# Norm rows read in the PSUM banks, and two more slots in the ring of expert rows, in a two-layer diffusion backbone

## Reference, cut to what matters

```
mod = silu(cond) @ w_mod + b_mod                  # 6 rows of 1024: sh1, sc1, g1, sh2, sc2, g2, one set for P, one for S
h   = layer_norm(x) * (1 + sc1) + sh1
mix = attention of three kinds (h @ w_in) @ w_out
x   = layer_norm(alpha * x + g1 * mix, ln1_g, ln1_b)
h   = layer_norm(x) * (1 + sc2) + sh2
ff  = peer_ffn(h)                                 # per token: 8 heads x top 16 = 128 experts of 16384
x   = layer_norm(alpha * x + g2 * ff, ln2_g, ln2_b)

def peer_ffn(h):                                  # u_tab, v_tab: 16384 x 1024
    q = h @ wq; s = q . keys; experts, gates = product-key top 16 of each head
    act = gelu(h . u_tab[experts])                # 128 dot products for each token
    return sum_k (gates * act)[k] * v_tab[experts[k]]
```

## Time and profile before

| | |
|---|---|
| median of 3 runs | 2485.88 us (2480.08 to 2488.46) |
| span of the profiled execution | 2660.3 us (its time beside the span is not shown) |
| TensorE, VectorE, GpSimd, ScalarE busy | 1716.3, 1616.4, 1491.3, 337.3 us |
| bytes moved | 980.68 MB, 369 GB/s over the span |
| of these, gathers and w_mod (queue 0) | 847.35 MB, 82.1% of 16 DMA engines' time |
| mean granted TensorE clock | 0.790 |

### The profile page before, as it was taken

One profiled execution on the slowest core, in us unless ns is written; L12 is line 12 of the kernel. 1 busy time (PEld: TensorE's weight loads), 2 busy tenths in 40 slices (PEclk: granted clock), 3 DMA queues, 4 the chain that ended last, 5 costly groups with the idle time before them and its releaser, 6 DMA issues.

```text
span 2660.3 us, 24559 instructions
## 1 busy us (share of the span) xinstructions
PE 1716.3 (65%) x8433; PEld 893.7 (34%) x8433; DVE 1616.4 (61%) x3949; ACT 337.3 (13%) x998; POOL 1491.3 (56%) x1583
## 2 busy tenths in 40 slices
PE   6886759676376666366577585867638667435556
PEld 4564514342143422222344342435214342000101
DVE  3266775676865673954467964547866566854441
ACT  1320013101120100002110101311112010000000
POOL 1105466655656465566455664555665666766664
PEclk8987877888578778687688797788757878777779
DMA  8969899999999999999899999889999999999997
GB/s 315 422 252 364 314 389 367 390 370 394 368 328 401 358 411 413 404 411 410 314 366 387 369 411 355 317 336 354 410 380 328 395 379 411 389 357 377 364 367 296
DMA packets 248333, 980.68 MB, mean 369 GB/s; under 512 B 28001, under 2 KB 29681, under 8 KB 232849
## 3 DMA queue, kind: packets, MB, share of 16 engines
q0 software_dynamic: 226944, 847.35, 82.1%
q1 hardware_dynamic: 19536, 130.80, 12.3%
q10 hardware_dynamic: 1728, 0.95, 0.1%
HBM read 976.47 MB, written 2.52 MB: 368 GB/s over the span
## 4 chain that ended last, share of the span: by engine, by line
PE 17%; issue 12%; POOL 9%; DMA 8%; another core or an unknown queue 8%; DVE 7%; ACT 1%; SPq 0%; DVEq 0%; ACTq 0%; POOLq 0%
POOL expert L660 9%; PE acc L968 6%; DMA expert<-in_experts,eidx_t 4%; DVE expert L1529 3%; PE mmb L911 2%; DMA expert<-in_experts,eidx 2%; PE mmb L779 2%; PE mmb L860 1%; PE ob L887 1%; DMA wt<-in_w_wq 1%; PE trb L867 1%; PE mmb L743 1%; ACT hT L1048 1%; DVE small L1216 0%
## 5 line engine op out<-in xcount | busy, mean ns | idle before, releaser
L660 POOL DMA_INDIRECT expert<-in_experts,eidx x768 | 736.1, 958 | 648.0 <-PE acc L968 261.2
L1529 DVE CUSTOM_DVE_ANT_0 expert<-expert,hb 128x1024 f32<-128x1024 f32 x768 | 904.3, 1218 | 268.1 <-DMA expert<-in_experts,eidx 211.2
L660 POOL DMA_INDIRECT expert<-in_experts,eidx_t x768 | 730.5, 951 | 329.7 <-issue 212.5
L968 PE MATMUL acc<-expert,strip 128*32 128x512 f32 x3072 | 710.8, 725 | 262.2 <-DMA expert<-in_experts,eidx_t 190.5
L968 PEld LDWEIGHTS acc<-expert,strip 128*32 128x32 f32 x3072 | 135.0, 123 | 737.5 <-DMA expert<-in_experts,eidx_t 399.5
L911 PE MATMUL mmb<-hT,wt 128*128 128x128 f32 x1472 | 211.8, 307 | 58.2 <-issue 31.4
L911 PEld LDWEIGHTS mmb<-hT,wt 128*128 128x128 f32 x1472 | 200.3, 220 | 86.7 <-issue 68.9
L769 PE MATMUL mmb<-wt,hT 128*128 128x244 f32 x736 | 178.6, 404 | 33.4 <-issue 12.9
L769 PEld LDWEIGHTS mmb<-wt,hT 128*128 128x128 f32 x736 | 152.8, 211 | 64.6 <-issue 35.3
L1399 DVE TENSOR_REDUCE neg_max<-mmb 128x1 f32<-128x384 f32 (+1 forms) x120 | 55.1, 466 | 165.1 <-PE mmb L860 83.5
L942 PE MATMUL trb<-ident,acts 128*128 128x128 f32 x24 | 9.6, 398 | 171.0 <-DVE acts L1549 100.9
(11 more groups left out here) (192 smaller groups left out, 1629.8 us busy)
## 6 DMA issues: line engine op xcount, KB each, us to landing
wt<-in_w_wq SPq DMA_DIRECT2D x46, 1152.0 KB
expert<-in_w_mod POOLq DMA_DIRECT2D x39, 1024.0 KB, 13.8
wt<-in_w_win SPq DMA_DIRECT2D x30, 976.0 KB
wt<-in_w_wout SPq DMA_DIRECT2D x24, 1024.0 KB
expert<-in_experts,eidx POOLq DMA_INDIRECT x768
expert<-in_experts,eidx_t POOLq DMA_INDIRECT x768
wt<-in_w_mod SPq DMA_DIRECT2D x8, 1024.0 KB
wt<-in_w_uq SPq DMA_DIRECT2D x6, 384.0 KB
```

Of the source, the lines that this page charges most:

```text
L660: pool.indirect_dma_start(expert[:, g % RING, :], None, table, bass.IndirectOffsetOnAxis(at, 0)).then_inc(landed[g % RING], 16)
L968: m = pe.matmul(acc[32 * i:32 * i + 32, cs], strip[:, q % 2, i, at:at + 32], expert[:, (g + i) % RING, cs], start=k < 4, stop=False, skip_ ...
L1529: v.tensor_tensor_reduce(expert[:, r, :], expert[:, r, :], hb[:], 1.0, 0.0, ALU.mult, ALU.add, dots[:, k:k + 1]).then_inc(dot_ready, 1)
```

## The change

Three things change together.

1. `rows` and `rows_used` are gone. A `row` step of a gain, a bias or the gate g1 leaves the row in the two `mmb` banks, which are now one tensor `mm2` of 1024 columns. VectorE waits for the matmuls (`mm_full`), reads `mm2` and then frees both banks (`row_used`). So each such row stands right ahead of its reader in the list, and gain and bias are read in two steps (`ln_x` 2 and 3, `fin` 2 and 3) with a row step in front of each.
2. The gate g2 of `fin` is still copied by ScalarE, now into `tmp`, in a `row` step at the end of the weave of its own block (`gate_row`).
3. The 8 KB a partition that `rows` took go to the ring: `RING` is 17. The ring of modulation weights keeps its 7 places.

The costs that space the gathers have the split steps and 0.5 for each row.

```diff
-RING = 15
+RING = 17
-RROWS = 2
...
 def weave(l, b, side, beside=()):
+    side = with_rows(side) + [("row", l, "", b, gate_row(l, b))]
...
+def gate_row(l, b):
+    return 16 * l + 10 + int(b > 0)
 def rows_wanted(x):
-                 {("ln_x", 0): (2,), ("ln_x", 2): (6, 7), ("fin", 0): (5,), ("fin", 2): (8, 9)}.get((kind, e), ()))
+                 {("ln_x", 0): (2,), ("ln_x", 2): (6,), ("ln_x", 3): (7,), ("fin", 2): (8,), ("fin", 3): (9,)}.get((kind, e), ()))
 def with_rows(steps):
-    (places each row as early as its bank, its buffer and its modulation allow)
+    return [y for x in steps for y in [("row", x[1], "", 0, j) for j in rows_wanted(x)] + [x]]
...
-        rows = sb("rows", [P, RROWS, D])
+        mm2 = ps("mmb", [P, D])
+        mmb = [mm2[:, 512 * i:512 * (i + 1)] for i in range(2)]
...
@@ ScalarE @@
-                if kind == "row":
-                    k = n("rows") - 1
-                    if k >= RROWS:
-                        act.wait_ge(rows_used, k - RROWS + 1)
-                    for half in range(2):
-                        mm_copy(rows[:, k % RROWS, half * 512:half * 512 + 512], lambda bk: bk[:], mm + half)
+                if kind == "row" and e != gate_row(l, b):
+                    n("mm_full", 2)
+                if kind == "row" and e == gate_row(l, b):
+                    act.wait_ge(idx_ready, n("gate", 0))
+                    if l == L - 1 and b > 0:
+                        act.wait_ge(y_ready, b)
+                    for u in (mm, mm + 1):
+                        half = u % 2
+                        mm_copy(tmp[:, half * 512:half * 512 + 512], lambda bk: bk[:], u)
@@ VectorE @@
+            def affine_gain(z):
+                link(v.scalar_tensor_tensor(out=z, in0=z, scalar=small[:, 28:29], in1=row(), op0=ALU.subtract, op1=ALU.mult))
+                row_used()
+            def affine_bias(dst, z):
+                link(v.scalar_tensor_tensor(out=dst, in0=z, scalar=small[:, 30:31], in1=row(), op0=ALU.mult, op1=ALU.add))
+                row_used()
             def row():
-                k = n("row") - 1
-                v.wait_ge(mm_free, at_row[k] + 2)
-                return rows[:, k % RROWS, :]
+                v.wait_ge(mm_full, at_row[n("row") - 1])
+                return mm2[:]
+            def row_used():
+                v.sem_inc(mm_free, 2)
...
-                        r = row()
+                        v.wait_ge(mm_free, at_gate + 2)
                         v.wait_ge(slot_done, SLOTS * (3 * l + b + 1))
-                        v.tensor_tensor(z, acc[:], r, ALU.mult).then_inc(acc_read, 1)
+                        v.tensor_tensor(z, acc[:], z, ALU.mult).then_inc(acc_read, 1)
```

More of the change, by code:

```diff
@@ L76 @@
 COST = {"mod": 2.8, "madd": 1.3, "cols": 1.5, "ln1": 5.5, "h_t": 2.5, "win": 6.8, "prep": (1.2, 7, 2.6, 3), "k_t": 2, "q_t": 4, "q_rope": 1.5,
-        "qm_t": 1, "cache_t": 2, "kv_mla": 5, "heads": 2, "mix": 1, "wout": 3.6, "ln_x": (2.5, 5.2, 2.5),
-        "ln_h": 5.2, "route": 1.5, "topk": 4.7, "pick": (4.4, 6.5, 4.4, 6.5), "fin": (1.3, 6.5, 2.5), "idx_t": 1}
+        "qm_t": 1, "cache_t": 2, "kv_mla": 5, "heads": 2, "mix": 1, "wout": 3.6, "ln_x": (2.5, 5.2, 1.3, 1.3), "row": 0.5,
+        "ln_h": 5.2, "route": 1.5, "topk": 4.7, "pick": (4.4, 6.5, 4.4, 6.5), "fin": (1.3, 6.5, 1.3, 1.3), "idx_t": 1}
 def cost_of(x):
@@ L152, in block_steps @@
     out += [("wout", l, s, b, n) for n in range(OUT_T)]
-    out += [("ln_x", l, s, b, i) for i in range(3)] + [("ln_h", l, s, b, 0), ("h_t", l, s, b, 2)]
+    out += [("ln_x", l, s, b, i) for i in range(4)] + [("ln_h", l, s, b, 0), ("h_t", l, s, b, 2)]
     for n in range(WQ_T + 1):
@@ L223, in fins @@
 def fins(l, b):
-    return [("fin", l, "", b, i) for i in range(3)]
+    return [("fin", l, "", b, i) for i in range(4)]
 def early_mod(x):
@@ L243, in plan @@
                   {"k_t": 1, "kv_mla": 1, "q_t": 1, "qm_t": 2, "heads": 0.45})
-    steps += prompt[mix:project] + [("madd", 0, "", 0, 2), ("cols", 0, "", 0, 1)] + fill(prompt[project:norm], s1[1:] + s2[1:] + rest[2:4], {"ln_x": 2})
+    steps += prompt[mix:project] + [("madd", 0, "", 0, 2), ("cols", 0, "", 0, 1)]
+    steps += with_rows(fill(prompt[project:norm], s1[1:] + s2[1:] + rest[2:4], {"ln_x": 1.5}))
     steps += fill(prompt[norm:cut], rest[4:] + [("madd", 0, "", 0, 3), ("cols", 1, "", 0, 0)], {"route": 1, "topk": 0.5, "pick": 4})
@@ L279, in rows_wanted @@
     return tuple(16 * l + (2 * r + st if r < 6 else 6 + r) for r in
-                 {("ln_x", 0): (2,), ("ln_x", 2): (6, 7), ("fin", 0): (5,), ("fin", 2): (8, 9)}.get((kind, e), ()))
+                 {("ln_x", 0): (2,), ("ln_x", 2): (6,), ("ln_x", 3): (7,), ("fin", 2): (8,), ("fin", 3): (9,)}.get((kind, e), ()))
 def with_rows(steps):
[L286 to L305, removed]
+    return [y for x in steps for y in [("row", x[1], "", 0, j) for j in rows_wanted(x)] + [x]]
+STEPS = plan()
 MODS = [x for x in STEPS if x[0] == "mod"]
+for at, step in enumerate(STEPS):
+    assert step[0] != "row" or all(STEPS.index(y) < at for y in MODS if y[1] == step[4] // 16 and y[3] == step[4] % 16 // 2)
 EARLY = sum(early_mod(x) for x in MODS)
 SUMS = sum(x[0] == "madd" for x in STEPS)
-MOD_RING = RING // 2
+MOD_RING = 7
 assert all(early_mod(x) for x in MODS[:EARLY])
@@ L455, in trunk_program @@
         acc = ps("acc", [P, D])
-        mmb = [ps(f"mmb{i}", [P, 512]) for i in range(2)]
+        mm2 = ps("mmb", [P, D])
+        mmb = [mm2[:, 512 * i:512 * (i + 1)] for i in range(2)]
         hb = ps("hb", [P, D])
@@ L1338, in _ @@
                 if kind == "row":
-                    at_row.append(mm)
+                    at_row.append(full)
+                    if e == gate_row(l, b):
+                        at_row.pop()
+                        at_gate = mm
                 if (kind, l, b, e) == ("prep", 0, 0, 0):
@@ L1440, in _ @@
                     if e == 2:
-                        affine(x[:, b, :], y, row, row)
-                        v.sem_inc(rows_used, 2)
+                        affine_gain(y)
+                    if e == 3:
+                        affine_bias(x[:, b, :], y)
                 if kind == "ln_h":
@@ L1568, in _ @@
                     if e == 2:
-                        affine(x[:, b, :], z, row, row)
-                        v.sem_inc(rows_used, 2)
+                        affine_gain(z)
+                    if e == 3:
+                        affine_bias(x[:, b, :], z)
                         if l == L - 1:
```

18 lines of the change are left out of this document (6 added, 12 removed).

## The result

The changed kernel takes 2495.18 us, median of 6 runs (2490.89 to 2505.98), against 2483.99 us of the kernel before, median of 6 (2480.08 to 2488.46): a ratio of 1.0054, 95% interval 1.0035 to 1.0074. It is slower by 0.5%; 1% faster was forecast. The time lies inside the range, the sign was wrong.

A forecast was written before the change was run, and what follows sets the result against it. Transfers were taken as nearly full, with 244 us lost in the gather stretch. Terms 22 + 30 + 2 - 9.5 - 12.6 - 2.1 gave 30 us saved of 2660.3, scaled by 0.934 to 28: 2458 us, range 2405 to 2505.

The forecast's parts named there:

- What bounds the kernel: Stretch with gathers: transfers nearly full, no engine is; 372 GB/s against 413 in a loaded window, 244 us lost.
- Ring, last stretch: From 2280 to 2640 us, 17 slots shorten some 9 waits by 2.49 us each: 22 us saved, at most 38.
- Ring, middle: 70 GpSimd waits on TensorE shrink, at most 174 us; a sixth counted: 30 us saved.
- Reads in PSUM: 30 VectorE reads move from SBUF to PSUM: durations unchanged, fewer gathers held up, 2 us saved (0 to 24).
- Gate: Gate row of `ln_x` goes behind a v group; VectorE starts 1.9 us later in 5 of 6 blocks: 9.5 us lost.
- bias: VectorE stands 2.1 us for each bias row: 12.6 us lost over six `ln_x`, 2.1 at the last `fin`.
- rival B: Chance 0.20: TensorE and VectorE wait for each other at every row, 83 us lost; 2539 us, mild form 2505.
- Gain: Gain rows of the norms: TensorE spreads each during the moments, 3.6 us of cover for 1.88, so 0 lost.
- The copied `fin` gate: ScalarE copies the `fin` gate into `tmp` ahead of time, as before into `rows`: 0, at most 7 us.
- Last bias: Bias row of the last `fin`: VectorE stands for semaphores and the row, 2.1 us lost.
- A: Rival, chance 0.15: the ring was deep enough already and rows cost little; ring 10, rows -10, 2486 us.
- C: Rival, chance 0.15: the ring is worth much more, all the transfers' idle time shrinks; 88 saved, scaled 82, 2404 us.

The follow-up runs named there:

- the second execution: The kernel before, nothing changed, profiled a second time: span 2480.6 us, median 2482.43 us.
- the changed kernel, again: The changed kernel, nothing altered, measured and profiled a second time: 2496.12 us, ratio 1.0041 to the kernel before.
- the best version: The changed kernel with the prompt block's three rows and the very last bias row copied to SBUF: 0.9980 and 0.9987 of the kernel before.
- the rows-first kernel: The changed kernel with only the step order at the prompt's norm altered, rows still in PSUM: 2488.58 us, ratio 1.0020 to the kernel before.

## Why the prediction was wrong, step by step

**What bounds the kernel: failed, and with it the sign.** "At 413 its 2460.5 x 372 = 915 MB would take 2216 us, so 244 us are lost in it" was true of that one execution. In a usual one the gather stretch runs at 405 GB/s and takes 2257 us, some 41 us above my 2216. I had seen that the execution was 174 us longer than the median of the runs, and scaled the sum by 0.934; but what makes it longer was exactly the loss that I gave the ring to win back: its first gather (211.3 us) and its end (12.1 us) are those of the second execution, and its middle is 2436.9 against 2257.4 us. The sum had to be made on what a 2486 us execution can have lost at most: 2460.5 - 174 - 2216 = 70 us, not 244.

**Ring, last stretch (22 us): measured 0.** 409 GB/s before and after. The sign that I had named, above 385 GB/s, came true and meant nothing, since it is true of the kernel before as well.

**Ring, middle (30 us): measured 7 to 10**, in the first and the fourth block; a sixth of the saved waits was still too much. GpSimd's waits on TensorE fell, from 262.8 to 225.8 us, as I had said; others grew in exchange (on VectorE's dots from 131.9 to 181.2). GpSimd feeds transfers that already run at their full rate, so its waits were not time.

**Reads in PSUM (2 us): durations right.** Gate 1.22, gain and bias 1.28 us. ScalarE's busy time fell by 36 us, from 337.3 to 301.2, at no effect. The gathers beside the reads were held up as I had said, and are no longer. The second execution of before and the changed kernel, again (timelines):

```profile
646.80 1.28 DVE L1232 SCALAR_TENSOR_TENSOR tmp<-tmp,small,rows 128x1024 f32<-128x1024 f32 x1
647.11 1.77 POOL L660 DMA_INDIRECT expert<-in_experts,eidx  x1 [0.30 <-DVE dots L1529]
```

```profile
657.27 1.28 DVE L1225 SCALAR_TENSOR_TENSOR tmp<-tmp,small,mmb 128x1024 f32<-128x1024 f32 x1
657.60 0.93 POOL L649 DMA_INDIRECT expert<-in_experts,eidx  x1 [0.30 <-DVE dots L1530]
```

In the whole of the first execution 26 gathers overlap a gain or bias read, and 8 of them take 1.15 to 2.00 us, 5.2 us above the usual 0.94 in total (I had guessed 12 us with the gate); in the other 32 overlap one and none takes over 0.94. It is time of GpSimd, which has slack; what it is worth in the kernel's time no run separates. One row of the prediction was misread: the gather of 1.65 us at 1779.08 ran beside L1435 (1778.68 to 1779.90), which reads two operands from SBUF in both kernels, and not beside L1434, which had ended at 1778.65.

**Gate (9.5) and bias (12.6 and 2.1): right that VectorE waits, wrong where it counts.** In the changed kernel's second execution VectorE waits for rows 53.7 + 32.3 + 22.7 = 108.7 us, against 32.4 before: 76 us more, close to rival B's 83. Yet in the whole middle this costs 4 to 10 us, as transfers go on beside it. I charged each of 6 blocks alike; most of the cost lies in the first and the last.

**Gain (0): the mis-sized term.** "TensorE spreads it during the moments [...] Cover 3.6 us for 1.88: 0" was read from the last norm, where nothing stands between. At the prompt norm two `h_t` steps and a `mod` step stand ahead of the row: 7.35 us of wait, in the one block that no gather covers. I had named this price for v rows that have not landed, and not for side steps. With gate and bias it makes 10.0 of the 16.0 us. The copied `fin` gate, also put at 0, cost 1.4 us of VectorE's wait in one execution of the changed kernel and none in the other.

**Last bias (2.1): measured 4.00**, because after its wait TensorE ran the row at half clock (3.75 us), which I had reckoned for the gate and not here.

**The sum as measured**, by the profiled executions: start +12.1 (10.0 by rows; 2.1 came before them, where the clock from 86 to 100 us differs), middle 0 (ring -7 to -10, rows +6 to +10; two executions of one kernel differ by 3.2 us there, 2257.3 and 2254.1), end +3.9: 16.0 us. The medians of the two kernels differ by 11.2 in the first runs and by 13.2 in the second; without the 2.1 us of clock the sum is 13.9.

**Rivals.** A was right on the ring in the last stretch and on what bounds the kernel: transfers. By the estimate that the prediction works out from the Trainium skill's rule (DMA: Bandwidth & Descriptors, anatomy of one DMA on the SWDGE path) slots 16 and 17 give nothing; the last two blocks agree with it, the middle as a whole, with 7 to 10 us, doesn't. In the first profile of the changed kernel a gather took 16.3 us from issue to landing (median; 4.5 the shortest), against the 3.2 us of one alone in that estimate. B was right on TensorE and VectorE waiting for each other, "TensorE sits idle for VectorE": 95.1 us in 10 waits; wrong on how much of it is time. C, a ring worth 96 us, fell: 7 to 10. That the measured time lies in the stated range is luck: the ring's term was over 40 us too large, and what the rows cost outside the middle was too small.

## What to carry to other kernels

Compare the profiled execution with the median before its waits are priced: if it is much longer (here 7%), the waits in it may be what is unusual about it, and scaling the sum doesn't mend that. In a kernel that is bound by transfers, price a change by where no transfer covers it, the start and the tail, and there walk each engine's queue step by step; in the middle, count bytes. Before an operand is moved from a buffer that is filled ahead to one that is filled on demand, look in each place at what stands in the producer's queue between the two.

## What the runs showed of the hardware that I had not expected

One execution of the unchanged kernel ran at 375 GB/s over 2240 us, another at 405, with the DMA share at 0.96 and 1.02: nearly as busy, but slower. None of the twelve other profiled executions shows it. The Trainium skill (HBM Reference, Specifications (TRN2)) says that two cores of a pair share their memory's bandwidth, so that each gets about 358 GB/s if both stream, and more if one streams alone. That would fit; no run here shows what the other core did, so the cause stays open.

TensorE's granted clock fell to its lower level at 86 us in some executions and not in others of the very same kernel: 0.53 and 1.00 in the window 86 to 100 us in the two runs of the best version. Where it stayed there until 127 us, the start took some 8 to 10 us more: the first gather of the changed kernel came at 233.6 us in the first profile (span 2504.2 us) and at 223.3 in the second, and the rows-first kernel lost 8.4 us before its norm. What decides it stays open.
